# A fused encoder step with a mixture of experts: a last stage shared out over three engines, and weight loads that let the first rows pass

## The reference, cut to what matters

```python
xp = xp + hier_moe(rmsnorm(xp, g_ffn_norm), ...)   # each row goes to 2 of 32 experts of width 128
y_prompt = rmsnorm(xp, g_final)                    # x * rsqrt(mean(x*x) + eps) * g_final
y_sample = rmsnorm(xs, g_final)
```

## Time and profile before

| | us |
|---|---|
| median of 3 runs (lowest, highest) | 957.94 (957.83, 959.48) |
| the profiled execution | 959.17 |
| its span | 957.3 |
| TensorE busy in the span | 829.1 |
| VectorE / ScalarE / GpSimd busy | 459.7 / 331.6 / 82.9 |

### The profile page before, as it was taken

The page is one execution under the profiler, slowest core; times in us unless marked ns, Lnnn a source line. Parts: engine busy times, 40 slices in busy tenths (PEclk is TensorE's granted clock), DMA queues, the critical chain, the costliest instruction groups (busy, mean ns, idle before and its releaser), DMA issues.

```text
span 957.3 us, 16435 instructions
## 1 busy us (share of the span) xinstructions
PE 829.1 (87%) x6131; PEld 716.0 (75%) x6131; DVE 459.7 (48%) x1142; ACT 331.6 (35%) x837; POOL 82.9 (9%) x138
## 2 busy tenths in 40 slices
PE   4999999999979889899999799999299999999500
PEld 3999999999957666677888588887276777777300
DVE  4731110111156656555776454663437555444377
ACT  5531111101146566655666343232022222222123
POOL 0000000000000000000000000000323334443100
PEclk9999999999979999999999799999589999999855
DMA  8211114110450411005000421120988999972195
GB/s 265 92 31 45 45 44 135 45 44 31 68 166 23 53 37 26 2 1 221 2 2 2 178 89 65 68 78 23 377 291 333 343 323 331 339 285 80 54 387 183
DMA packets 62498, 124.61 MB, mean 130 GB/s; under 512 B 13387, under 2 KB 34723, under 8 KB 62435
## 3 DMA queue, kind: packets, MB, share of 16 engines
q1 hardware_dynamic: 53219, 105.91, 32.9%
q0 software_dynamic: 9216, 17.85, 5.2%
HBM read 108.72 MB, written 30.73 MB: 146 GB/s over the span
## 4 chain that ended last, share of the span: by engine, by line
PE 75%; DVE 11%; ACT 5%; DMA 4%; issue 4%; SPq 0%; POOLq 0%; DVEq 0%; POOL 0%; ACTq 0%
PE ps L1517 34%; PE ps L1865 11%; PE ps L1871 5%; PE ps L1744 4%; PE ps L1858 3%; PE ps L1626 2%; DVE big L1124 2%; PE ps L1610 2%; PE ps L1720 2%; PE ps L1731 2%; PE ps L1641 2%; PE ps L1804 2%; ACT big L757 1%; DMA out_y_prompt<-big 1%; PE ps L1682 1%
## 5 line engine op out<-in xcount | busy, mean ns | idle before, releaser
L1517 PE MATMUL ps<-wg_hi,xl 128*128 128x256 f32 x576 | 163.4, 284 | 0.3 <-DVE wg_lo L996 0.3
L1517 PE MATMUL ps<-wg_hi,xh 128*128 128x256 f32 x576 | 163.0, 283 | 0.0
L1517 PE MATMUL ps<-wg_lo,xh 128*128 128x256 f32 x576 | 163.0, 283 | 0.0
L1517 PEld LDWEIGHTS ps<-wg_hi,xl 128*128 128x128 f32 x576 | 110.5, 192 | 0.5 <-issue 0.5
L1517 PEld LDWEIGHTS ps<-wg_lo,xh 128*128 128x128 f32 x576 | 110.6, 192 | 0.0
L1517 PEld LDWEIGHTS ps<-wg_hi,xh 128*128 128x128 f32 x576 | 110.5, 192 | 0.0
L1865 PEld LDWEIGHTS ps<-fox,work 128*128 128x128 f32 x320 | 60.6, 190 | 19.4 <-issue 12.2
L1865 PE MATMUL ps<-fox,work 128*128 128x256 f32 x320 | 72.5, 379 | 2.0 <-DVE work L1415 2.0
L1415 DVE COPY work<-ps 128x512 f32<-128x512 f32 x32 | 22.1, 692 | 94.8 <-PE ps L1858 94.7
L1000 DVE COPY fox<-ps 128x256 f32 (+1 forms) x27 | 11.4, 422 | 101.8 <-PE ps L1517 101.8
L1517 PE MATMUL ps<-w_out_h,oTl 128*128 128x512 f32 x144 | 58.9, 409 | 1.5 <-DVE oTl L1258 1.5
(11 more groups left out here) (295 smaller groups left out, 1770.1 us busy)
## 6 DMA issues: line engine op xcount, KB each, us to landing
fox<-in_w_gate SPq DMA_DIRECT2D x20, 512.0 KB, 4.6
fox<-in_w_up SPq DMA_DIRECT2D x20, 512.0 KB, 6.3
fox<-in_w_down SPq DMA_DIRECT2D x20, 512.0 KB, 6.5
work<-in_w_in SPq DMA_DIRECT2D x8, 1024.0 KB, 5.5
fox<-y_rows SPq DMA_DIRECT2D x16, 512.0 KB, 7.1
h_rows<-big SPq DMA_DIRECT2D x9, 512.0 KB, 2.7
work<-in_x_prompt SPq DMA_DIRECT2D x8, 512.0 KB, 4.6
fox<-in_w_out SPq DMA_DIRECT2D x1, 4096.0 KB, 14.0
```

Of the source, the lines that this page charges most:

```text
L1517: mm = pe.matmul(out, xs[a](c), ws[b](c), start=(c + k == 0), stop=(c == C - 1 and k == 2))
```

## The change

Four edits. In the last stage the square goes to a scratch area of its own (`squares`), `fin` has four buffers, ScalarE multiplies the row by the inverted root (an `activation` Copy with a per-row scale), GpSimd multiplies it in place by `g_final`, and VectorE keeps the two additions and the reciprocal. On ScalarE the square of tile i + 1 stands ahead of the scaling of tile i. `g_final` is loaded early in the expert stage into a buffer of its own. The first four gathers take their index straight from the table, with no copy and no wait for it. SP issues experts 2 and 3, then waits until the gathers of tiles 0 and 1 have landed, and only then issues 4 to 7.

```diff
-        fin = [cut(big, free0 + 7 * D + u * D, D) for u in range(2)]
+        g_fin = cut(big, free0 + 2 * D, D)
+        squares = cut(swa, 0, D)
+        fin = [cut(swa, D + u * D, D) for u in range(4)]
...
             sp.wait_ge(s["om_done"], NT)
-            for k in range(2, NSLOT - 1):
+            for k in range(2, 4):
+                expert(k)
+            for k in range(2):
+                sp.wait_ge(g_in[k], 16)
+            for k in range(4, NSLOT - 1):
                 expert(k)
...
             gate_up(NSLOT, 0)
+            sp.wait_ge(s["hT_done"], 2 * NT)
+            sp.wait_ge(s["h_out_a"], 16 * 5)
+            sp.wait_ge(s["h_out_b"], 16 * 4)
+            sp.dma_start(g_fin, row(t["g_final"], D)).then_inc(s["g_late_in"], 16)
...
             sp.wait_ge(s["experts_done"], 1)
-            sp.dma_start(g1[:, :], row(t["g_final"], D)).then_inc(s["g_late_in"], 16)
...
             for tt in range(4):
-                gather(tt, tt)
+                pool.sem_inc(s["idx_set"], 1)
+                pool.sem_inc(s["pool_went"], 1)
+                pool.indirect_dma_start(
+                    out=hg[tt], out_offset=None, in_=h_dram,
+                    in_offset=bass.IndirectOffsetOnAxis(ap=ids[:, 2 * tt:2 * tt + 1], axis=0),
...
+            pool.wait_ge(s["g_late_in"], 64)
+            for i in range(NT):
+                rows = P if i < SAMPLE else DEC
+                pool.wait_ge(s["f_mid"], i + 1)
+                pool.tensor_tensor(fin[i % 4][0:rows, :], fin[i % 4][0:rows, :], g_fin[0:rows, :], ALU.mult).then_inc(s["f_fin"], 1)
...
-            norm_f(0, 0, P)
-            norm_f(1, 1, P)
-            with act.Fori(1, NP_T // 2) as j:
-                for u in range(2):
-                    norm_f(j * 2 + u, u, P)
-            norm_f(8, 0, DEC)
+            norm_f(0)
+            for i in range(NT):
+                if i + 1 < NT:
+                    norm_f(i + 1)
+                rows = P if i < SAMPLE else DEC
+                act.wait_ge(s["f_rstd"], i + 1)
+                if i >= 4:
+                    act.wait_ge(f_out[i % 4], i // 4 * 16)
+                act.activation(fin[i % 4][0:rows, :], o_all[0:rows, i, :], ACT.Copy,
+                               scale=st[0:rows, 8 + i % 4:9 + i % 4]).then_inc(s["f_mid"], 1)
...
-            def scale_f(i, u, rows):
+            def invert_f(i, rows):
                 dve.wait_ge(s["f_rms"], i + 1)
-                dve.reciprocal(st[0:rows, 4 + u:5 + u], st[0:rows, 2 + u:3 + u]).then_inc(s["f_rstd"], 1)
-                dve.wait_ge(s["f_rstd"], i + 1)
-                dve.scalar_tensor_tensor(out=fin[u][0:rows, :], in0=o_all[0:rows, ds(i, 1), :].rearrange("p a n -> p (a n)"),
-                                         scalar=st[0:rows, 4 + u:5 + u], in1=g1[0:rows, :],
-                                         op0=ALU.mult, op1=ALU.mult).then_inc(s["f_fin"], 1)
-
-            dve.wait_ge(s["g_late_in"], 64)
+                if i >= 4:
+                    dve.wait_ge(s["f_mid"], i - 3)
+                dve.reciprocal(st[0:rows, 8 + i % 4:9 + i % 4], st[0:rows, 2 + i % 2:3 + i % 2]).then_inc(s["f_rstd"], 1)
```

More of the change, by code:

```diff
@@ L292, in build @@
             v_idx v_g v_w v_gT v_gTc v_gu v_e v_s v_hid v_hT v_hTc v_dn v_y v_out experts_done
-            f_acc f_stat f_rms f_rstd f_fin f_out_a f_out_b""".split()
+            f_acc f_stat f_rms f_rstd f_fin f_mid""".split()
         s = {n: sem(n) for n in names}
@@ L301, in build @@
         y_out = [sem(f"y_out{u}") for u in range(4)]
+        f_out = [sem(f"f_out{u}") for u in range(4)]
         y_in = [sem(f"y_in{u}") for u in range(4)]
@@ L545, in load_y, with store @@
                 sp.dma_start(yb[u][0:rows, :], y_dram[ds(i * P + TOK, rows), :]).then_inc(y_in[u], 16)
-            def store(i, u):
+            def store(i):
+                rows = t["y_prompt"].rearrange("a s d -> (a s) d")[i * P:(i + 1) * P, :] if i < SAMPLE else t["y_sample"].rearrange("a s d -> (a s) d")
                 sp.wait_ge(s["f_fin"], i + 1)
-                sp.dma_start(t["y_prompt"].rearrange("a s d -> (a s) d")[ds(i * P, P), :], fin[u]).then_inc(s["f_out_b" if u else "f_out_a"], 16)
+                sp.dma_start(rows, fin[i % 4][0:P if i < SAMPLE else DEC, :]).then_inc(f_out[i % 4], 16)
             for i in range(4):
@@ L556, in _ @@
                     load_y(i + 4, i % 4, P if i + 4 < SAMPLE else DEC)
[L557 to L562, removed]
+                store(i)
+            for u in range(4):
+                sp.wait_ge(f_out[u], 16 * len(range(u, NT, 4)))
         @block.gpsimd
@@ L612, in _ @@
             for tt in range(4):
-                gather(tt, tt)
+                pool.sem_inc(s["idx_set"], 1)
[3 more added lines that the diff above has]
+                    in_offset=bass.IndirectOffsetOnAxis(ap=ids[:, 2 * tt:2 * tt + 1], axis=0),
+                    bounds_check=TOK - 1, oob_is_err=False).then_inc(g_in[tt], 16)
             pool.wait_ge(s["gT_done"], 2)
@@ L953, in _, with norm_f @@
             act.wait_ge(s["experts_done"], 1)
-            def norm_f(i, u, rows):
+            def norm_f(i):
+                u, rows = i % 2, P if i < SAMPLE else DEC
                 act.wait_ge(s["f_acc"], i * 2 + 2)
[L958 to L961, removed]
+                act.activation(squares[0:rows, :], o_all[0:rows, i, :], ACT.Square, accum_out=st[0:rows, u:u + 1]).then_inc(s["f_stat"], 1)
                 act.wait_ge(s["f_stat"], i + 1)
+                if i >= 2:
+                    act.wait_ge(s["f_rstd"], i - 1)
                 act.activation(st[0:rows, 2 + u:3 + u], st[0:rows, u:u + 1], ACT.Sqrt, bias=eps[0:rows, 0:1], scale=1.0 / D).then_inc(s["f_rms"], 1)
-            norm_f(0, 0, P)
-            norm_f(1, 1, P)
-            with act.Fori(1, NP_T // 2) as j:
-                for u in range(2):
-                    norm_f(j * 2 + u, u, P)
-            norm_f(8, 0, DEC)
+            norm_f(0)
[8 more added lines that the diff above has]
+                               scale=st[0:rows, 8 + i % 4:9 + i % 4]).then_inc(s["f_mid"], 1)
         @block.vector
@@ L1493, in _ @@
                     add_y(i + 1, (i + 1) // 4, (i + 1) % 4, P if i + 1 < SAMPLE else DEC)
-                scale_f(i, i % 2, P if i < SAMPLE else DEC)
+                invert_f(i, P if i < SAMPLE else DEC)
         @block.tensor
```

## The result

The changed kernel takes 961.69 us (median of 6 runs, 961.04 to 963.16) against 957.27 (6 runs, 955.32 to 959.48) of the kernel before: ratio 1.0049, interval 1.0033 to 1.0065, so 3.2 to 6.2 us slower. A gain of 2.1 us had been forecast.

What follows compares the result with a forecast made beforehand. Bound: TensorE's chain from the first gather's landing, then VectorE and store landings in the last stage, transfers near their limit. Head -3.7 and last stage +1.6 gave -2.1 us: 957.94 to 955.8 us, range 949.5 to 959.5.

Steps and rivals of the forecast that it cites:

- The gather sets the start, its landing 4.3 us after 686.8, head -3.7: Start of expert stage: first gather lands sooner without weights ahead, transposes begin at 691.1 instead of 694.74, 3.7 us earlier.
- The margin of the late weights: Expert stage: expert 4's weights, issued later, are in by 699 and needed at 720, a margin of 20 us.
- the clock's rise with the work: Expert stage: TensorE's clock rises at the same distance from its work, keeping all 3.7 us; otherwise a loss of 1.9.
- The first addition 2.2 us sooner after the first load: Last stage start: with final weights loaded early, VectorE's first addition starts at 912.3 instead of 914.55.
- Multiply 2.1 us, exclusion: Last stage: each GpSimd multiply takes 2.1 us and takes turns with VectorE's additions; this case's chance 0.50.
- I add 1.2 us for handovers: Last stage: nine handovers of about 0.13 us between VectorE and GpSimd, added to 34.2 us of alternating work, to 955.7.
- The last store needs what it needed: End of program: 3.25 us from the end of the arithmetic to the end of the span, as before, giving 958.9.
- Last stage +1.6: Last stage as a whole: 1.6 us longer, ending at 958.9 in place of 957.3.
- No exclusion: Rival, chance 0.30: VectorE and GpSimd run side by side, transfers pace the last stage; stage -3.6, together -7.3, 950.6 us.
- A dear multiply: Rival, chance 0.10: with exclusion, a GpSimd multiply of 2.9 us makes the last stage 7.2 us longer, 963.0 us.

Runs made afterwards that it cites:

- e8: Kernel before with only the first four gathers taken straight from the table, weights in the old order: 957.56 us, ratio 1.0009 to before.
- e9: Kernel before plus a one-element-per-partition GpSimd memset at the start of the last stage: 955.72 us, ratio 0.9992 to before.
- e1: Kernel before with the new head alone (direct gathers, experts 4 to 7 after the first two gathers landed), old last stage: 952.68 us, ratio 0.9958.
- e4: Changed kernel with GpSimd's multiply replaced by a memset of the same tile, product by final weights left out: 951.09 us, ratio 0.9940 to before.
- e6: Changed kernel with GpSimd's multiply replaced by a copy of the tile onto itself, product by final weights left out: 951.57 us, ratio 0.9952 to before.
- e7: Changed kernel with ScalarE scaling tile i before it squares tile i + 1: 961.14 us, ratio 1.0061 to before.
- e2: Changed kernel with the old head, so the last stage alone is new: 964.37 us, ratio 1.0074 to before.
- e5: Kernel before plus a one-element-per-partition GpSimd memset after the last tile: 960.29 us, ratio 1.0043 to before.
- e11: Changed kernel with the last tile's product (64 rows) on VectorE instead of GpSimd: 960.21 us, ratio 1.0038 to before.

## Why the prediction was wrong, point by point

- *The gather sets the start, its landing 4.3 us after 686.8, head -3.7.* Right in mechanism, a little too large: landing 4.65, 3.2 us less from the table to the transposes, the expert stage 3.4 shorter than in before's profile and 2.4 to 2.7 than in those of e8 and e9, e1 faster by 2.7 to 5.4 us. The missing copy alone gives nothing (e8).
- *The margin of the late weights, the clock's rise with the work.* Right: share 1.03 from 700 to 720 and no wait for weights, clock up 8 us after the first transposes.
- *The first addition 2.2 us sooner after the first load.* Measured 1.9 (from SP's first issue 5.3 us, before 7.2), and not isolated by an experiment.
- *Multiply 2.1 us, exclusion.* Right, the multiply 0.2 too short. It is 2.3 us long and costs a meeting addition 1.96, and e4 and e6 show that the reads exclude each other. The Trainium skill (SBUF — State Buffer, "Who interferes with whom") is borne out on both sides: an addition with two SBUF inputs stayed at 1.28 us beside a writer and went to 1.99 and 3.24 beside readers. "Blocked for the whole of the first" holds within 0.2 us: 3.47 - 1.28 = 2.19 beside a multiply of 2.35 (e7). The estimate of 2.25 us from the Trainium skill (GPSIMD Engine Reference, "Elementwise — side-by-side cycle accounting") was nearer to the multiply's 2.3 than mine.
- *"I add 1.2 us for handovers", 35.4 us from GpSimd's start to its end.* 37.0 us in the changed kernel's profile (916.58 to 953.60), 2.6 of them the idle time ahead of multiply 7, which I had overlooked; 35.2 in e2's (921.55 to 956.78), which hasn't got it. That 35.4 comes so near to e2's is partly luck: nine multiplies at 2.34 are 2.2 us more than at 2.1, but the 1.2 us for handovers don't show, and a met addition grows by less than the whole multiply.
- *"The last store needs what it needed, 957.3 - 954.05 = 3.25 us from the end of the arithmetic."* This step failed. It holds where VectorE works last and not where GpSimd does: 5.6 us from its last instruction, 2.4 more (e5, e9, e11).
- *Last stage +1.6.* The profiles have +6.3 (62.5 against 56.2): 1.6 forecast, 2.4 from the end, 1.6 from GpSimd's stretch, 0.3 from its start, 0.4 from the first load. In e2's profile (+4.4) GpSimd's stretch adds nothing. What remains, and what made the error larger in the times than in the profiles, is the base: the product was weighed against 56.2 us, of which some 3 were a late store of this one execution (53.0 to 53.5 in e1, e8, e9). Against these the stage is 7 to 9.5 us longer (60.6 in e2, 62.5 in the changed kernel); timed, e2 is 5.6 to 8.7 slower. So of the 5.9 us between 955.8 and 961.69 the base gives some 3 and the end of the program 2.4: the second step that failed is the last stage's +1.6, weighed against the 56.2 us of a single profile.
- *The rivals.* "No exclusion" fell by e4 and e6. "A dear multiply" ended on the right side for a wrong reason: the multiply was nearly as cheap as forecast, 2.3 us where this rival asked for over 2.5, and what turned the sign was not on the list.
- *The range.* 949.5 to 959.5 did not hold 961.69; it had no room for an end of the program that depends on which engine works last, nor for the base.

## What to carry to other kernels

Before work goes to GpSimd, ask what VectorE reads meanwhile: two engines that exclude each other add up, and 1.28 us taken off VectorE came back as 1.96. If GpSimd computes in the last 6 us of a program, count what its end adds (5.6 us from its last instruction here), or give its last piece to another engine and measure. When several transfers start together, issue first the one that the next stage waits for, and let the bulk wait for its landing. And weigh a stage by more than one profile: a late store in one execution was worth more than the whole forecast.

## What the runs showed of the hardware that was not expected

- With GpSimd at work near its end the program ended 5.5 to 5.6 us after GpSimd's last compute instruction in all seven such profiles, even if that was a memset of 0.10 us (e5); with GpSimd long idle SP waits only 0.2 us past the last landing (e9).
- An excluded instruction is recorded as a long one (3.24 for 1.28 us), with no idle time and no releaser. The view of waits therefore says nothing of the exclusion: the busy time of VectorE rose from 459.7 to 462.3 us although it had nine products less.
- Without the index copy the first four gathers of the changed kernel followed each other at 1.3 to 1.5 us (685.86, 687.38, 688.68, 689.98) instead of 2.1 to 2.3, and this alone was worth nothing that could be measured (e8).
